# Two engines' score steps moved in the order of the attention stages: ScalarE's exponentials 2.5 steps later, VectorE's maxima 2.5 steps sooner

## The chip, the core and the metric

The kernel is one program on one core of a Trainium2 chip. It is written out by hand: each engine has its own list of instructions, and semaphores alone keep them in step. The metric is the device time in microseconds (us), the median of several runs. In the profile the engines are PE (TensorE matmuls), PEld (TensorE weight loads), DVE (VectorE), ACT (ScalarE), POOL (GpSimd) and SP (SyncE, which issues most DMAs).

## What is computed

Two transformer-like blocks run one after the other on 512 tokens of width 1024, everything in float32 accuracy. The first has sliding-window attention (8 heads), block attention (8 heads; with two key blocks its top-k takes every past block, so it is plain causal attention with a bias), a merge of both, and an MLP. The second has a short convolution, a gated MLP, "forgetting" attention with 16 causal heads, and a second gated MLP. For the change only the two attention stages matter. Their core is, for each head and each tile of 128 queries:

```python
s = einsum(q, k) * scale + bias          # -inf above the diagonal or out of the window
m = max(s, axis=-1)                      # first 8 heads: also max with the head's sink
p = exp(s - m)
p = p / sum(p)                           # first 8 heads: sum(p) + exp(sink - m)
o = einsum(p, v)
```

Stage 1 holds the 8 window heads (kind "swa") and 8 causal heads of the first block, stage 2 the 16 causal heads of the second.

## The kernel before

**Accuracy.** Matmuls run in the type float32r. Each operand is split into a high half (rounded by an ACT copy, `a_hi`) and a low half (the rest, by a DVE subtraction, `d_lo`, `low_half` at L1627), and each product is three matmuls: high by high, high by low, low by high (`mm3`, L598; L599 to L601). So whatever TensorE writes and later reads again passes through ACT first and then DVE.

**One head.** A head has four query tiles. For tile i TensorE writes the scores to one of two PSUM banks (`score` at L724; in stage 2 a fourth matmul at L744 adds the forget gates). DVE adds the bias or mask and takes the row maximum in one instruction (L1663), then makes the negative maximum column (L1668). ACT takes the exponential in place and sums it (L1206). When all four tiles are done, "norm": DVE takes the reciprocal of the sums (L1678) and scales tiles 0 to 2 (L1681), ACT scales tile 3 (L1230). Then come the turnings "t": TensorE transposes 128x128 blocks of probabilities to one of two other banks (L756), ACT makes the high half (L1238), DVE the low half (L1629 through `low_half`). A causal head has four turnings (t.0 of four blocks, t.1 of three, t.2 of two, t.3 of one), a window head two. Then "v": TensorE multiplies them by the values (L772 to L774). Last "out": the head's result is split by ACT (L1244) and DVE (L1629) in the place of its queries. A causal tile i is 128(i+1) keys wide, so its exponential and its maximum go over 128 to 512 columns.

**Banks.** A score bank is free for the score after the next when DVE has taken the maximum (event "top"). A turning bank is free for the turning after the next when DVE has the low half (event "pt"). So t.0 of a head waits for the low half of t.2 of the head before it.

**The order.** `attention_steps` (L209) makes one list of steps for each stage, and TensorE, ACT, DVE and POOL each walk through it and do what in it concerns them: `STEPS1` (L285) and `STEPS2` (L287). Heads overlap: while head n is multiplied, the scores of later heads and the turnings of head n+1 are already made. The order of one head is written out in tables:

```python
SEQ = {"causal": ["v0", "t2", "v1", "t3", "+t0", "v2", "+t1", "v3"],
       "swa": ["v0", "v1", "+t0", "v2", "v3", "+t1"]}
LEAD = {"causal": [8, 8, 8, 9, 10, 11, 12, 12], "swa": [10, 11, 12, 12, 12, 13]}
```

A "+" is a turning of the next head, and LEAD says how many score tiles have been started by then. Between these steps stand units of other work for TensorE (`fill`): projections of the keys, values and gates needed later, each unit one `mm3` of 512 columns or two of 256 (L599 to L601). They end in "evac" steps (ACT's high half, DVE's low half of a whole bank; in between L1185, L1201). "piece" steps convert a quarter of a weight slot, ACT the high part (L1118), POOL the low part (L2042). "start" steps are POOL's (the bias DMA of a head in stage 1, the gate operand at L2100 in stage 2). In stage 2 the work for filling is used up in head 12, so the last heads run without any. A stretch of the list for a causal head with filling reads:

```text
t8.3  score10.0  unit  t9.0  score10.1  unit  v8.2  score10.2  evac  take  unit  piece0
t9.1  score10.3  start12  unit  piece1  v8.3  unit  piece2  v9.0  unit  piece3  norm10  t9.2
```

and of the last ones, without:

```text
norm13  t12.2  out11  v12.1  t12.3  score14.0  t13.0  score14.1  v12.2  score14.2  t13.1
score14.3  v12.3  v13.0  norm14  t13.2  out12  v13.1  t13.3  score15.0  t14.0 ...
```

Units, takes and v are TensorE's alone. Of a "score" step ACT does the exponential, DVE the maximum, TensorE the four matmuls. The engines' loops over the list are the functions `attention` in `program_act` (L1212), `program_dve` (L1684), `program_pe` (L830) and `program_pool` (L2110).

Of the kernel before, what the change touches and what calls it, by code (L numbers as in the profile page):

```python
# [191 lines left out]
def job_units(job):  # L192

    kind, slot = job
    if kind == "o":
        yield ("idle",)
        yield ("take", slot)
        for i in range(2):
            for kt in range(5):
                yield ("unit", job, i, kt)  # L200
        return
    yield ("take", slot)
    for i in range(2):
        for u in range(8):
            yield ("unit", job, i, u)
        yield ("evac", job, i)


def attention_steps(kinds, jobs, quota, first):  # L209


    steps, pieces = [], []
    n_heads = len(kinds)

    def one_unit():
        for job in jobs:
            for step in job_units(job):
                if step[0] == "take":
                    while pieces:
                        steps.append(pieces.pop(0))  # L220
                    steps.append(step)
                    if step[1] + 1 in PIECED and step[1] + 1 >= first:
                        pieces.extend(("piece", step[1] + 1, c) for c in range(4))
                elif step[0] == "evac":
                    steps.append(step)
                else:
                    steps.append(step)
                    yield

    units = one_unit()  # L230

    def fill(n):
        for _ in range(n):
            next(units, None)
            if pieces:
                steps.append(pieces.pop(0))

    started, tiled = [0], [0]

    def start(n):  # L240
        while started[0] < min(n, n_heads):
            steps.append(("start", started[0]))
            started[0] += 1

    def tiles(n):
        while tiled[0] < min(n, 4 * n_heads):
            steps.append(("score", tiled[0] // 4, tiled[0] % 4))
            tiled[0] += 1
            start(tiled[0] // 4 + 2)

    start(2)
    for n in range(8):
        tiles(n + 1)
        fill(1)
    steps.append(("norm", 0))
    fill(1)
    for g in (0, 1):
        steps.append(("t", 0, g))
        fill(1)
    for n, kind in enumerate(kinds):  # L260
        nxt = n + 1 < n_heads
        seq = SEQ[kind]
        extra = max(0, quota[n] - len(seq))
        for at, step in enumerate(seq):
            if at == NORM[kind] and nxt:
                steps.append(("norm", n + 1))
            if at == 2 and n:
                steps.append(("out", n - 1))
            if step[0] != "+":
                steps.append((step[0], n, int(step[1])))  # L270
            elif nxt:
                steps.append((step[1], n + 1, int(step[2])))
            lead = LEAD[kind][at]
            tiles(4 * n + (lead if nxt and kinds[n + 1] == kind else min(lead, 12)))
            fill(2 if at < extra else (1 if at < quota[n] else 0))
    steps.append(("out", n_heads - 1))
    for _ in units:
        pass
    steps.extend(pieces)
    return steps  # L280

# [61 lines left out]
def build(nc, a, out_t, scratch):  # L345
    with ExitStack() as ctx:
# [164 lines left out]
        stage_steps = {1: STEPS1, 2: STEPS2}  # L511
# [564 lines left out]
        def prob(st, h, i):  # L1076
            hd = heads[st][h]
            n, off = score_span(hd, i)[1], OFF[hd["kind"]][i]
            return sp_b[h % 2][:, off:off + n]
# [24 lines left out]
        def program_act(act, on):  # L1104
# [8 lines left out]
            def piece(n, c):  # L1113
                s = slice(512 * c, 512 * c + 512)
                on.wait_ge(raw_in[n % NRAW], "landed", n)
                if n >= NW:
                    on.wait_ge(mm, "slot", n - NW)
                act.activation(WH[:, n % NW, s], raw[:, n % NRAW, s], ACT.Copy).then_inc(w_hi.sem, w_hi.up("slot", n, c))  # L1118
# [68 lines left out]
            def evacuate(name, n, i, bank):  # L1187
                if name[0] == "q":
                    queries(name[:2], 2 * int(name[2]) + i, bank, "job", n, i)
                elif name[0] == "g":  # L1190
                    k = 2 * int(name[1]) + i
                    on.wait_ge(mm, "job", n, i)
                    act.activation(sg_b[k], psum[bank][:, :], ACT.Copy).then_inc(a_evac.sem, a_evac.up("gate", k))
                elif name[-2] == "k":
                    kv_free(on, name)
                    keys(name, bank, n, i)
                else:
                    kv_free(on, name)
                    on.wait_ge(mm, "job", n, i)
                    src, hi, lo = places_of_values(name, bank, i)  # L1200
                    act.activation(hi, src, ACT.Copy).then_inc(a_hi.sem, a_hi.up(name, i))  # L1201
# [9 lines left out]

            def attention(st, tiles_done, turns_done):  # L1212
                tile, turn = tiles_done, turns_done
                for step in stage_steps[st]:
                    what = step[0]
                    if what == "take":
                        slot[0] += 1
                    elif what == "piece":
                        piece(step[1], step[2])
                    elif what == "evac":  # L1220
                        (name, n), i = step[1:]
                        evacuate(name, n, i, 6 + tile % 2)
                        tile += 1
                    elif what == "score":
                        exponentials(st, step[1], step[2])
                    elif what == "norm":
                        h = step[1]
                        on.wait_ge(a_exp, "exp", st, h, 3)
                        on.wait_ge(d_soft, "recip", st, h)
                        act.activation(prob(st, h, 3), prob(st, h, 3), ACT.Copy, scale=stats(h)[4][:, 3:4]).then_inc(  # L1230
                            a_exp.sem, a_exp.up("scaled", st, h, 3))
                    elif what == "t":
                        h, g = step[1:]
                        src, hi, lo = weights_turned(st, h, g, 2 + turn % 2)
                        turn += 1
                        on.wait_ge(mm, "turned", st, h, g)
                        turned_free(on, st, h, g)
                        act.activation(hi, src, ACT.Copy).then_inc(a_hi.sem, a_hi.up("pt", st, h, g))  # L1238
                    elif what == "out":
                        h = step[1]  # L1240
                        hd = heads[st][h]
                        r = slice(hd["r0"], hd["r0"] + 64)
                        on.wait_ge(mm, "sum", st, h, 3)
                        act.activation(hd["q"][0][r, :], psum[4 + h % 2][r, :], ACT.Copy).then_inc(  # L1244
                            a_hi.sem, a_hi.up("out", st, h))
# [243 lines left out]
        def program_dve(dve, on):  # L1489
# [193 lines left out]

            def attention(st, tiles_done, turns_done):  # L1684
                tile, turn, scored = tiles_done, turns_done, 0
                for step in stage_steps[st]:
                    what = step[0]
                    if what == "take":
                        slot[0] += 1
                    elif what == "evac":  # L1690
                        (name, n), i = step[1:]
                        evacuate(name, i, 6 + tile % 2)
                        tile += 1
                    elif what == "score":
                        score(st, step[1], step[2], scored % 2)
                        scored += 1
                    elif what == "norm":
                        normalise(st, step[1])
                    elif what == "t":
                        h, g = step[1:]  # L1700
                        src, hi, lo = weights_turned(st, h, g, 2 + turn % 2)
                        turn += 1
                        low_half(lo, src, hi, "pt", st, h, g)
                    elif what == "out":
                        h = step[1]
                        hd = heads[st][h]
                        r = slice(hd["r0"], hd["r0"] + 64)
                        low_half(hd["q"][1][r, :], psum[4 + h % 2][r, :], hd["q"][0][r, :], "out", st, h)
# [719 lines left out]
```

## Time and profile before

| what | value |
|---|---|
| median of 3 runs | 2031.24 us (2031.15 to 2031.51) |
| the profiled execution | 2031.23 us, of which the span of its instructions 2029.4 us |
| TensorE matmuls busy | 1954.0 us, 96% |
| VectorE, ScalarE, GpSimd busy | 57%, 37%, 16% |
| stage 1 of attention | about 76 to 245 us of the span |
| stage 2 of attention | about 1405 to 1595 us |

The span is the time from the first to the last instruction in the trace; the rest of the execution's time, some 2 us, lies around it. In the rows an engine's idle time stands in front of an instruction together with what ended it: `[1.05 <-ACT t L1238]` means that it stood still 1.05 us until the ACT instruction of L1238 was done.

### The profile page before, as it was taken

The numbers are of one execution on the slowest core, as the hardware profiler recorded it, in microseconds if no ns is written. First come the engines' busy times: TensorE is split into PE (matmuls) and PEld (weight loads), VectorE is DVE, ScalarE is ACT, GpSimd is POOL, SyncE is SP. The second block draws the span as 40 slices with busy tenths as digits, with TensorE's granted clock in tenths as the row PEclk, the third lists the DMA queues.
The fourth block names the chain that finished last, engine by engine and source line by source line (L and its number), as shares of the span: only waits on it lengthen the run. The fifth ranks groups of instructions, "written<-read, shape, count | busy, mean of one in ns | idle before, by whom it ended". The sixth has DMA issues, their size and how long they took to land.

```text
span 2029.4 us, 22573 instructions
## 1 busy us (share of the span) xinstructions
PE 1954.0 (96%) x9134; PEld 1607.5 (79%) x9134; DVE 1163.7 (57%) x1841; ACT 757.0 (37%) x1141; POOL 333.2 (16%) x293
## 2 busy tenths in 40 slices
PE   4999999999999999999999999999999899999997
PEld 3888888778888887887888888868888678888885
DVE  6566565576676745666655654565666554432445
ACT  4556632352223234223422122374565352222223
POOL 4422211021111102003100000147222130000002
PEclk9999999999999999999999999999999999999998
DMA  9422366266565424432654523232111122323321
GB/s 330 138 82 63 114 232 236 83 219 215 210 219 196 166 85 169 161 108 80 237 195 169 187 87 100 86 123 88 43 42 43 64 91 95 104 83 104 98 90 42
DMA packets 126121, 267.57 MB, mean 132 GB/s; under 512 B 4463, under 2 KB 33151, under 8 KB 126016
## 3 DMA queue, kind: packets, MB, share of 16 engines
q1 hardware_dynamic: 121056, 248.59, 35.9%
q0 software_dynamic: 4960, 17.53, 2.4%
q8 instruction: 72, 1.18, 0.2%
q14 instruction: 33, 0.27, 0.0%
HBM read 261.84 MB, written 8.45 MB: 133 GB/s over the span
## 4 chain that ended last, share of the span: by engine, by line
PE 66%; ACT 5%; DVE 4%; POOL 2%; issue 1%; DMA 1%; ACTq 0%; SPq 0%; DVEq 0%; POOLq 0%
PE ps L599 21%; PE ps L601 21%; PE ps L600 21%; DVE t L1629 1%; ACT t L1164 1%; ACT t L1160 1%; ACT t L1206 1%; ACT t L1118 1%; PE ps L756 1%; POOL t L2227 1%; DVE t L1663 1%; DVE t L1601 0%; DVE t L1554 0%; DMA x_keep<-t 0%; POOL t L2042 0%
## 5 line engine op out<-in xcount | busy, mean ns | idle before, releaser
L599 PE MATMUL ps<-t 128*128 128x512 f32 (+1 forms) x2504 | 969.5, 387 | 17.5 <-DVE t L1629 4.3
L601 PE MATMUL ps<-t 128*128 128x512 f32 (+1 forms) x2504 | 962.8, 385 | 0.0
L600 PE MATMUL ps<-t 128*128 128x512 f32 (+1 forms) x2504 | 962.0, 384 | 0.0
L599 PEld LDWEIGHTS ps<-t 128*128 128x128 f32 x2504 | 471.4, 188 | 119.0 <-DVE t L1494 6.5
L1494 DVE TENSOR_TENSOR t<-t 128x2048 fp32r<-128x2048 f32 x133 | 305.0, 2294 | 441.9 <-ACT t L1111 441.9
L601 PEld LDWEIGHTS ps<-t 128*128 128x128 f32 x2504 | 470.9, 188 | 98.9
L600 PEld LDWEIGHTS ps<-t 128*128 128x128 f32 x2504 | 471.2, 188 | 94.2 <-issue 1.0
L1111 ACT ACTIVATE t<-t 128x2048 fp32r<-128x2048 f32 x133 | 254.3, 1912 | 618.6 <-PE ps L601 611.1
L1554 DVE SCALAR_TENSOR_TENSOR t<-ps,t 128x512 f32<-128x512 f32 x184 | 132.6, 748 | 91.5 <-PE ps L601 82.7
L1506 DVE CUSTOM_DVE_ANT_0 t<-t 128x1024 f32<-128x1024 f32 x144 | 175.5, 1260 | 10.3 <-DMA t<-in_ada_t 3.6
L1629 DVE TENSOR_TENSOR t<-ps,t 64x512 fp32r<-64x512 f32 (+4 forms) x183 | 103.8, 577 | 103.4 <-ACT t L1238 48.7
L2042 POOL TENSOR_TENSOR t<-t 128x512 fp32r<-128x512 f32 x88 | 117.1, 1346 | 221.9 <-ACT t L1118 221.9
L2071 POOL COPY t<-t 128x512 f32<-128x512 f32 x4 | 2.8, 710 | 849.1 <-DVE t L1554 801.6
L1206 ACT ACTIVATE t<-t 128x256 f32<-128x256 f32 (+3 forms) x128 | 69.4, 542 | 118.2 <-DVE t L1668 117.1
L1629 DVE TENSOR_TENSOR t<-t 128x512 fp32r<-128x512 f32 (+1 forms) x93 | 71.1, 767 | 73.1 <-ACT t L1392 30.7
L2178 POOL TENSOR_TENSOR t<-t 128x512 f32<-128x512 f32 x32 | 46.3, 1446 | 282.2 <-ACT t L1331 282.2
L1134 ACT ACTIVATE t<-t 128x512 f32<-128x512 f32 x56 | 35.0, 631 | 89.9 <-DVE t L1554 88.2
L756 PE MATMUL ps<-t 128*128 128x128 f32 x296 | 53.2, 279 | 12.9 <-DVE t L1629 11.4
L1392 ACT ACTIVATE t<-t 128x512 fp32r<-128x512 f32 x44 | 27.8, 632 | 99.9 <-DVE t L1907 99.9
L1663 DVE CUSTOM_DVE_ANT_0 t<-ps,t 128x256 f32<-128x256 f32 (+3 forms) x128 | 58.4, 456 | 8.8 <-PE ps L744 6.1
L756 PEld LDWEIGHTS ps<-t 128*128 128x128 f32 x296 | 37.0, 141 | 25.4 <-DVE t L1629 15.1
L1160 ACT ACTIVATE t<-t 128x512 fp32r<-128x512 f32 x56 | 45.2, 807 | 27.7 <-DVE t L1618 14.1
(170 smaller groups left out, 1561.8 us busy)
## 6 DMA issues: line engine op xcount, KB each, us to landing
t<-in_ada SPq DMA_DIRECT2D x48, 1024.0 KB, 6.0
t<-in_gate SPq DMA_DIRECT2D x22, 1024.0 KB, 5.0
t<-in_up SPq DMA_DIRECT2D x22, 1024.0 KB, 5.1
t<-in_down SPq DMA_DIRECT2D x22, 1024.0 KB, 5.1
t<-in_w_in SPq DMA_DIRECT2D x17, 1024.0 KB, 5.7
t<-in_w_mlp_in SPq DMA_DIRECT2D x16, 1024.0 KB, 5.4
t<-in_w_mlp_out SPq DMA_DIRECT2D x16, 1024.0 KB, 5.1
t<-in_ada_t POOLq DMA_DIRECT2D x13, 1024.0 KB, 6.0
```

The source lines that it names most:

```text
L599: pe.matmul(o, wh, xh, start=first, stop=False)
L600: pe.matmul(o, wh, xl, start=False, stop=False)
L601: return pe.matmul(o, wl, xh, start=False, stop=last)
L756: ins = pe.transpose(psum[bank][:, blocks[n]], sp_b[h % 2][:, col:col + P], ident)
L1111: act.activation(WH[:, n % NW, :], raw[:, n % NRAW, :], ACT.Copy).then_inc(w_hi.sem, w_hi.up("slot", n))
L1206: act.activation(prob(st, h, i), prob(st, h, i), ACT.Exp, bias=neg[:, i:i + 1], accum_out=sm[:, i:i + 1]).then_inc(a_exp.sem, a_exp.up("ex ...
L1494: dve.tensor_tensor(WL[:, n % NW, :], raw[:, n % NRAW, :], WH[:, n % NW, :].bitcast(F), ALU.subtract).then_inc(w_lo_d.sem, w_lo_d.up("slot ...
L1506: ins = dve.tensor_tensor_reduce(out=v, in0=v, in1=cs, scale=1.0, scalar=0.0, op0=ALU.mult, op1=ALU.add, accum_out=mods[:, col + i:col + i ...
L1554: return dve.scalar_tensor_tensor(out=X[k], in0=psum[bank][:, :], scalar=gate, in1=X[k], op0=ALU.mult, op1=ALU.add)
L1629: dve.tensor_tensor(lo, src, hi.bitcast(F), ALU.subtract).then_inc(d_lo.sem, d_lo.up(*event))
L1663: dve.tensor_tensor_reduce(out=prob(st, h, i), in0=psum[bank][:, 0:n], in1=bias_of(st, h, i), scale=1.0, scalar=LOW, op0=ALU.add, op1=ALU. ...
L2042: pool.tensor_tensor(WL[:, n % NW, s], raw[:, n % NRAW, s], WH[:, n % NW, s].bitcast(F), ALU.subtract).then_inc(w_lo_p.sem, w_lo_p.up("slo ...
```

## The change

Both engines' loops walk through a sorted copy of the list. A score step counts 2.5 places later for ScalarE and 2.5 sooner for VectorE; every other step keeps its number, and TensorE and GpSimd keep the old list.

```diff
+def moved(steps, by):
+
+    return [step for _, step in sorted(enumerate(steps), key=lambda e: e[0] + by.get(e[1][0], 0))]
...
             def attention(st, tiles_done, turns_done):
                 tile, turn = tiles_done, turns_done
-                for step in stage_steps[st]:
+                for step in moved(stage_steps[st], {"score": 2.5}):
                     what = step[0]
...
             def attention(st, tiles_done, turns_done):
                 tile, turn, scored = tiles_done, turns_done, 0
-                for step in stage_steps[st]:
+                for step in moved(stage_steps[st], {"score": -2.5}):
                     what = step[0]
```

The first of the two is in `program_act`, the second in `program_dve`. The same instructions with the same operands are issued.

## Rows read from the trace of the kernel before

**Rows 1.** The page, busy time of each engine over the span

```profile
PE 1954.0 (96%) x9134; PEld 1607.5 (79%) x9134; DVE 1163.7 (57%) x1841; ACT 757.0 (37%) x1141; POOL 333.2 (16%) x293
```

**Rows 2.** Waits of PE, 76 to 245 us: us in total, times, longest

```profile
PE ps L756 <- DVE t L1629: 1.9, 3, 1.0
PE ps L756 <- DVE t L1681: 1.4, 3, 0.6
PE ps L738 <- DVE t L1663: 1.1, 2, 0.6
PE ps L772 <- DVE t L1629: 1.0, 2, 0.7
```

**Rows 3.** Waits of PE, 1405 to 1595 us

```profile
PE ps L756 <- DVE t L1629: 9.5, 8, 2.5
PE ps L738 <- DVE t L1663: 1.8, 2, 1.0
PE ps L599 <- DVE t L1629: 1.6, 1, 1.6
PE ps L772 <- DVE t L1629: 1.2, 3, 0.6
```

**Rows 4.** Waits of PE, 1562 to 1592 us, the last heads

```profile
PE ps L756 <- DVE t L1629: 5.5, 3, 2.5
```

**Rows 5.** Waits of ACT and of DVE, 1405 to 1595 us

```profile
ACT t L1206 <- DVE t L1668: 62.8, 53, 2.3
...
DVE t L1629 <- ACT t L1238: 27.9, 41, 1.5
```

**Rows 6.** Timeline of the last heads: start us, us, instruction, [idle before <-releaser]

```profile
1565.64 0.66 PE L756 MATMUL ps<-t 128*128 128x128 f32 x4 [1.00 <-DVE t L1629]
1569.32 0.50 PE L738 MATMUL ps<-t 128*128 128x512 f32 x1 [0.95 <-DVE t L1663]
1575.27 0.66 PE L756 MATMUL ps<-t 128*128 128x128 f32 x4 [2.02 <-DVE t L1629]
1584.63 0.99 PE L756 MATMUL ps<-t 128*128 128x128 f32 x4 [2.49 <-DVE t L1629]
...
1565.77 1.02 DVE L1629 TENSOR_TENSOR t<-ps,t 64x512 fp32r<-64x512 f32 x2 [0.19 <-ACT t L1244]
1568.23 0.69 DVE L1629 TENSOR_TENSOR t<-ps,t 128x512 fp32r<-128x512 f32 x1 [1.05 <-ACT t L1238]
1571.26 0.56 DVE L1629 TENSOR_TENSOR t<-ps,t 128x384 fp32r<-128x384 f32 x1 [1.15 <-ACT t L1238]
1571.73 0.68 DVE L1663 CUSTOM_DVE_ANT_0 t<-ps,t 128x512 f32<-128x512 f32 x1
1573.71 0.88 DVE L1681 TENSOR_SCALAR t<-t 128x128 f32<-128x128 f32 x3
```

**Rows 7.** Timeline of PE, two stalls in heads with filling

```profile
1486.78 0.44 PE L756 MATMUL ps<-t 128*128 128x128 f32 x2 [1.20 <-DVE t L1629]
...
1521.10 0.66 PE L756 MATMUL ps<-t 128*128 128x128 f32 x4 [0.58 <-DVE t L1629]
```

**Rows 8.** Timeline of DVE, 1479 to 1485 us, ahead of the first of them

```profile
1479.83 1.41 DVE L1629 TENSOR_TENSOR t<-ps,t 64x512 fp32r<-64x512 f32 x2 [1.26 <-ACT t L1185]
...
1482.10 0.68 DVE L1663 CUSTOM_DVE_ANT_0 t<-ps,t 128x512 f32<-128x512 f32 x1
...
1484.07 1.92 DVE L1681 TENSOR_SCALAR t<-t 128x128 f32<-128x128 f32 x3
```

**Rows 9.** Timeline of DVE in a window head of stage 1, low half of out

```profile
123.74 0.68 DVE L1629 TENSOR_TENSOR t<-ps,t 64x512 fp32r<-64x512 f32 x1 [1.58 <-ACT t L1244]
```

**Rows 10.** A stretch: us, busy (x count) of five engines, PEclk, DMA, GB/s

```profile
1586.00:1588.00 2.00, 2.00 (x10) 1.90 (x9) 1.23 (x2) 0.74 (x2) 0.00 (x0) 0.50 0.00 0
```

**Rows 11.** Line 1681 (ns min/median/max), and timeline of POOL beside that scaling

```profile
L1681 DVE TENSOR_SCALAR t<-t x96: 285/348/1468, 85.0 to 1583.5; 128x256 f32<-128x256 f32 x40, 128x128 f32<-128x128 f32 x32, 128x384 f32<-128x384 f32 x24
...
1484.43 3.94 POOL L2042 TENSOR_TENSOR t<-t 128x512 fp32r<-128x512 f32 x3 [1.31 <-ACT t L1118]
```

## The prediction

> **What bounds the kernel now.** I read the page's busy times first, then who TensorE waits for in the two attention stages, then the timeline of each engine around those waits. TensorE matmuls cover 1954.0 of 2029.4 us [rows 1], so only 75 us in the whole kernel are open, and the change touches the stretches 76 to 245 us (stage 1) and 1405 to 1595 us (stage 2). There TensorE waits for VectorE and next to nothing else: 5.4 us in stage 1 [rows 2] and 14.1 us in stage 2 [rows 3], of which 5.5 us are one kind of stall in the last three heads, where no projection work is left to fill in [rows 4]. That is 19.5 us at most for any reordering. VectorE and ScalarE are not full in these stages, they wait for each other: in stage 2 ScalarE stands 62.8 us before exponentials (L1206) until VectorE has the negative maximum (L1668), and VectorE 27.9 us before low halves (L1629) until ScalarE has the high half (L1238) [rows 5]. Both queues are in order, so a step that waits holds all that stands behind it.
>
> **The ping-pong, in the last heads.** [rows 6] shows one cycle of a head without filling, from one "t.0" turning on TensorE to the next: 1565.64, then 1575.27, 9.63 us. On VectorE the low half of t.0 (1568.23) waits 1.05 us for a high half that ScalarE does only behind the exponential of tile 0, and the maxima of tiles 1 and 2 stand behind it. The same again at tile 3: the low half of t.1 (1571.26) waited 1.15 us, maximum 3 follows at 1571.73, then exponential, reciprocal and scaling (1573.71, 0.88 us), the low half of t.2, and the next turning. TensorE stalls 0.95 us for a score bank (1569.32) and 2.02 us for that last step.
>
> **What the change moves.** Nothing is added or removed; no DMA moves (SP's loads, POOL's loads and its order are untouched). Steps are sorted by place, a score step counted 2.5 later for ScalarE and 2.5 sooner for VectorE, while TensorE and POOL keep their order. Most of what is passed is TensorE's alone, so the order of an engine changes only where a step of its own is passed. Written out from the plan: on ScalarE 26 of 64 exponentials in stage 1 (passing 11 weight pieces, 6 t, 6 evac, 3 norm) and 30 of 64 in stage 2 (17 t, 11 evac, 2 pieces); on VectorE 41 maxima in stage 1 (33 t, 8 norm, 7 out) and 42 in stage 2 (42 t). A causal head's VectorE order goes from t.3, s.0, t.0, s.1, s.2, t.1, s.3 to s.0, t.3, s.1, t.0, s.2, s.3, t.1; ScalarE's becomes t.3, t.0, s.0, s.1, t.1, s.2, s.3 in the last heads. Each engine then has work that is ready while the other does the half it needs.
>
> **Last heads, step by step** (differences of starts in [rows 6]). Take the same turning at 1565.64. VectorE's low half of "out" starts at 1565.77 and maximum 3 at 1571.73, 5.96 us later. In between lie the two waits (1.05 and 1.15) and the low half of t.1 (0.48 to the next start), and all three now come off the path to maximum 3, as the high halves are done while VectorE takes maxima: 5.96 - 2.68 = 3.28, so VectorE could take it at 1569.05. Score 3 has to be there: its bank is now freed before TensorE asks, the 0.95 us go, it starts at 1568.4, and four 512-column matmuls take it to about 1569.5 (0.50 for the first, 0.23 between starts: an estimate). Maximum 3 at 1569.5 for 1571.73 is 2.2 us sooner. What follows it, 3.5 us to the turning, stays as it is. The cycle becomes 7.4 us for 9.63, with 0.8 us of stall left for 2.02. Two such cycles (the second ends at 1584.63 behind 2.49 us of stall) give 4.4 us. The 1.00 us in front of them loses about 0.5, as in the filled heads below. Term: -4.9.
>
> **Filled causal heads.** The stalls are at the same step, t.0 behind the low half of t.2: 1.20 us at 1486.78 and 0.58 at 1521.10 [rows 7], five stalls and 4.0 us before the last heads (9.5 less 5.5 us, 8 less 3) [rows 3, 4]. In [rows 8] maximum 3 starts at 1482.10 behind the low half of t.1. Put first, it starts when the two low halves of the evacuation are through (1479.83 + 1.41), 0.86 us sooner, and its exponential, the scaling and t.2 move along. So 1.20 becomes 0.34, another long one alike, and the shorter ones nearly vanish. Term for stage 2: -3.1. In stage 1's causal heads the three stalls of this kind sum to 1.9 us, the longest 1.0 [rows 2]; by the same 0.86 they come to 0.2: -1.7.
>
> **Window heads of stage 1.** Two stalls of a score bank, 1.1 us [rows 2], arise as maximum 0 stands behind the low half of t.1; passing it is worth the 0.48 of [rows 6] to each: -1.0. Three stalls for the scaling, 1.4 us: maximum 1 now goes ahead of norm and costs it some 0.6, but maximum 3 goes ahead of out and t.0. The low half of out waited 1.58 us, until 123.74, for ScalarE [rows 9], and out and t.0 take about 1.2 on VectorE before maximum 3: that much sooner is all that comes after. I take half of the 1.4: -0.7.
>
> **What it costs.** 75 low halves of turned weights come later by a maximum and its column (0.68 us for the widest alone [rows 6], less than half for the narrowest), and may wait for a score first. The weighted products need them; the stalls of that kind are 1.0 and 1.2 us now [rows 2, 3]. The cover is TensorE's own projection work (a unit of three 512-column matmuls) between t and v. In the last heads, where it is missing, the low half of t.1 lands at about 1570.8, just as TensorE reaches the product that needs it. I put +0.4, bounds 0 and +3. Weight pieces go ahead of exponentials in 13 places: they only come sooner. Work behind attention (output projection, the reload of x, the next weight slot) starts from its end and shifts with it: 0.
>
> **The clock.** The granted clock is 0.50 in 1586 to 1588 [rows 10], the lower of its two levels (1.2 of 2.4 GHz), right behind the longest stall, 2.49 us [rows 6]; behind the one of 2.02 us four transposes take 0.66 us, so it was still high. With that stall near 0.8 the fall may not come. The four transposes take 0.99 us there for 0.66, half as much again; over 3.8 us of work at that pace it is at most 1.3 us. Bounds 0 and -1.3; as no row decides, half: -0.6.
>
> **Sum.** -4.9 - 3.1 - 1.7 - 1.0 - 0.7 + 0.4 - 0.6 = -11.6. The profiled execution took 2031.23 us (span 2029.4), the median is 2031.24, so no correction: **2019.6 us**.
>
> **A rule that speaks against it.** VectorE's scaling (L1681, three tiles) takes 1.92 us at 1484.07, where POOL's pieces run (3.94 us from 1484.43), and 0.88 us at 1573.71 without them [rows 6, 8, 11]. The Trainium skill, "SBUF — State Buffer", section "Who interferes with whom", has VectorE and GpSimd contending for a shared port pair as an exclusive lock in such cases. Hanging on that, the trace agrees in kind: the op lengthens only beside POOL.
>
> **The rivals.**
> (a) *The stalls re-form, 14%.* TensorE arrives sooner, and the same chain (exponential 3, reciprocal, scaling, t.2) ends last again with less gained. For: the scaling chain is untouched, 3 us of it. Against: it starts from maximum 3, which the order does bring forward. Only half the last-head term would stay: 2031.2 - 2.5 = 2028.7.
> (b) *Scalings fall beside POOL, 5%.* The 96 instructions go from 285 to 1468 ns [rows 11], and by the timeline 13 of the 32 scalings are long now. If the 12 short ones outside the first and last heads became long, 12 x 1.04 (1.92 less 0.88) = 12.5 on the chain: 2019.6 + 12.5 = 2032. Against: pieces and scaling hang on the same exponential and move together. It is the skill's lock rule that would drive it.
> (c) *Slower, 7%.* VectorE stands before a maximum whose score TensorE has not written (its queue is in order), with a low half behind it that v or a turning needs. Price: maximum and column, about 0.6, plus a score of four matmuls, about 0.7: 1.3 us. It decides where the cover between t and v is under 1.3 us, less than two units. If half of the 32 heads lost 1 us against now, +16 less the last heads' gain: 2031.2 + 16 - 4.9 = about 2042; with a quarter of them 2034, which I take.
> (d) *Forecast, 74%.* The step orders follow from the sort, so the change does what it says; that case gets no chance of its own.
>
> **Numbers.** A difference of about 0.2% (4 us) is what can be told from none. Below 2027.2: forecast and a fifth of (a), 0.77; within: the rest of (a) and (b), 0.16; above: 0.07. Floor: all 19.5 us and 1.3 of clock would be 2010; with half of the forecast's leftover stalls gone too, 2014. Upwards the range goes into (a): 2028.5.
>
> **What would show it.** Right: ScalarE's wait at L1206 for L1668 in stage 2 well under 62.8 us and VectorE's at L1629 for L1238 under 27.9, VectorE's waits at L1663 for scores up; the last heads' cycle near 7.4 us; L738 stalls gone; stalls at L756 for L1629 of stage 2 under 4. Wrong: new stalls at L772 for L1629, waits of TensorE equal to now, or L1681 longer in the mean.

## The result, and the profile after

The changed kernel takes **2011.57 us** in the median (2010.2 to 2012.88, 4 runs) against 2031.2: a ratio of 0.9902, 95% interval 0.9888 to 0.9916, so 19.6 us or 1% faster. The forecast was 2019.6, and 2014.0 to 2028.5 does not hold it. The direction and the mechanism of the moves were right; the gain was two thirds larger than forecast, as each stall was priced too low.

First where it lies. The span fell from 2029.4 to 2010.3 us. Taking each stage from its first score matmul to its last product by values, stage 1 went from 167.1 us (75.8 to 242.9) to 159.6, stage 2 from 185.0 (1406.0 to 1591.0) to 173.7; all the rest of the kernel together lost 0.4. The rows are those of the two lines for each stage, with the first and the last start; only the matmul rows stand here. The kernel before, lines 738 and 774:

```profile
L738 PE MATMUL ps<-t x64: 277/364/496, 75.8 to 230.7; 128*128 128x256 f32 x48, 128*128 128x384 f32 x8, 128*128 128x512 f32 x8
L774 PE MATMUL ps<-t x64: 273/281/397, 88.0 to 242.9; 128*128 128x256 f32 x32, 128*128 128x128 f32 x16, 128*128 128x512 f32 x8, 128*128 128x384 f32 x8
...
L738 PE MATMUL ps<-t x64: 277/364/504, 1406.0 to 1578.7; 128*128 128x256 f32 x32, 128*128 128x384 f32 x16, 128*128 128x512 f32 x16
L774 PE MATMUL ps<-t x64: 273/336/419, 1423.6 to 1591.0; 128*128 128x512 f32 x16, 128*128 128x384 f32 x16, 128*128 128x256 f32 x16, 128*128 128x128 f32 x16
```

The changed kernel, lines 743 (first matmul of a score) and 779 (last of a product), in stage 1 and in stage 2:

```profile
L743 PE MATMUL ps<-t x64: 277/362/487, 74.6 to 222.0; 128*128 128x256 f32 x48, 128*128 128x384 f32 x8, 128*128 128x512 f32 x8
L779 PE MATMUL ps<-t x64: 273/281/397, 86.8 to 234.2; 128*128 128x256 f32 x32, 128*128 128x128 f32 x16, 128*128 128x512 f32 x8, 128*128 128x384 f32 x8
...
L743 PE MATMUL ps<-t x64: 277/364/482, 1398.6 to 1562.2; 128*128 128x256 f32 x32, 128*128 128x384 f32 x16, 128*128 128x512 f32 x16
L779 PE MATMUL ps<-t x64: 273/308/397, 1416.3 to 1572.3; 128*128 128x512 f32 x16, 128*128 128x384 f32 x16, 128*128 128x256 f32 x16, 128*128 128x128 f32 x16
```

(Lines of the changed kernel stand five further down than those of the kernel before.) TensorE's waits in stage 1 (74 to 236 us), where [rows 2] had 5.4 us. The first is of the projections ahead of it:

```profile
PE ps L889 <- ACT t L1287: 0.8, 1, 0.8
PE ps L777 <- DVE t L1634: 0.3, 1, 0.3
PE ps L761 <- DVE t L1686: 0.2, 1, 0.2
```

and in stage 2 (1398 to 1575 us), where [rows 3] had 14.1:

```profile
PE ps L777 <- DVE t L1634: 2.5, 7, 0.6
PE ps L761 <- DVE t L1634: 2.2, 3, 1.2
PE ps L604 <- DVE t L1634: 1.6, 1, 1.6
```

The stalls before turnings (9.5 us) are down to 2.2, those for a score bank are gone, and those before products have doubled from 1.2 to 2.5: the price of low halves that come later. ScalarE's and VectorE's own waits in the same stretch, against [rows 5]:

```profile
ACT t L1243 <- PE ps L761: 29.5, 32, 1.6
ACT t L1211 <- DVE t L1673: 22.3, 44, 2.3
...
DVE t L1668 <- PE ps L749: 31.2, 45, 1.8
DVE t L1634 <- ACT t L1243: 7.9, 18, 0.9
```

ScalarE waited 62.8 us for negative maxima and now 22.3; VectorE waited 27.9 for high halves and now 7.9. In their place both wait for TensorE, ScalarE 29.5 us for turnings and VectorE 31.2 for scores. TensorE's own waits for VectorE are down from 14.1 to 6.3 us in the same stretch.

Last, one cycle of the last heads, to be read beside [rows 6]:

```profile
1559.93 0.66 PE L761 MATMUL ps<-t 128*128 128x128 f32 x4 [0.77 <-DVE t L1634]
...
1566.96 0.66 PE L761 MATMUL ps<-t 128*128 128x128 f32 x4 [1.23 <-DVE t L1634]
...
1560.53 0.27 DVE L1668 CUSTOM_DVE_ANT_0 t<-ps,t 128x128 f32<-128x128 f32 x1
1560.92 0.28 DVE L1634 TENSOR_TENSOR t<-ps,t 128x128 fp32r<-128x128 f32 x1
1561.12 0.41 DVE L1668 CUSTOM_DVE_ANT_0 t<-ps,t 128x256 f32<-128x256 f32 x1
1561.64 0.68 DVE L1634 TENSOR_TENSOR t<-ps,t 128x512 fp32r<-128x512 f32 x1
1562.24 0.55 DVE L1668 CUSTOM_DVE_ANT_0 t<-ps,t 128x384 f32<-128x384 f32 x1
1563.41 0.69 DVE L1668 CUSTOM_DVE_ANT_0 t<-ps,t 128x512 f32<-128x512 f32 x1 [0.43 <-PE ps L749]
1564.22 0.55 DVE L1634 TENSOR_TENSOR t<-ps,t 128x384 fp32r<-128x384 f32 x1
1565.40 0.88 DVE L1686 TENSOR_SCALAR t<-t 128x128 f32<-128x128 f32 x3
```

(VectorE's read-outs and negative maxima between these rows, and the reciprocal, are left out.) Maxima and the low halves of t.0 and t.1 alternate without a wait for ScalarE, maximum 3 waits only for its score, and the cycle is 7.03 us for 9.63.

### The profile page after: what moved, and what is told of

Its sections match the earlier page's. It is cut to its first block, busy times and chain, and to the rows that moved or that the text cites. A ratio compares the mean times of both kernels' runs of the same rounds, so it can differ in the third digit from the quotient of the medians.

```text
span 2010.3 us, 22573 instructions
## 1 busy us (share of the span) xinstructions
PE 1947.9 (97%) x9134; PEld 1605.5 (80%) x9134; DVE 1166.7 (58%) x1841; ACT 758.5 (38%) x1141; POOL 333.2 (17%) x293
## 3 DMA queue, kind: packets, MB, share of 16 engines
HBM read 261.84 MB, written 8.45 MB: 134 GB/s over the span
## 4 chain that ended last, share of the span: by engine, by line
PE 69%; ACT 4%; DVE 3%; POOL 2%; issue 1%; DMA 1%; ACTq 0%; SPq 0%; DVEq 0%; POOLq 0%
PE ps L604 21%; PE ps L606 21%; PE ps L605 21%; ACT t L1165 1%; ACT t L1169 1%; PE ps L761 1%; POOL t L2232 1%; DVE t L1634 1%; PE ps L743 1%; PE ps L744 1%; PE ps L749 1%; PE ps L745 1%; PE ps L777 0%; DVE t L1606 0%; DVE t L1559 0%
## 5 line engine op out<-in xcount | busy, mean ns | idle before, releaser
L604 PEld LDWEIGHTS ps<-t 128*128 128x128 f32 x2504 | 470.8, 188 | 117.8 <-DVE t L1499 6.5
L606 PEld LDWEIGHTS ps<-t 128*128 128x128 f32 x2504 | 470.9, 188 | 98.9
L605 PEld LDWEIGHTS ps<-t 128*128 128x128 f32 x2504 | 471.0, 188 | 94.4 <-issue 1.0
L2047 POOL TENSOR_TENSOR t<-t 128x512 fp32r<-128x512 f32 x88 | 116.9, 1346 | 203.1 <-ACT t L1123 203.1
L1634 DVE TENSOR_TENSOR t<-ps,t 64x512 fp32r<-64x512 f32 (+4 forms) x183 | 104.3, 574 | 39.2 <-ACT t L1243 14.8
L1243 ACT ACTIVATE t<-ps 128x512 fp32r<-128x512 f32 (+1 forms) x112 | 50.0, 448 | 50.0 <-PE ps L761 49.2
```

What stands on the lines that cost most here:

```text
L604: pe.matmul(o, wh, xh, start=first, stop=False)
L605: pe.matmul(o, wh, xl, start=False, stop=False)
L606: return pe.matmul(o, wl, xh, start=False, stop=last)
L1634: dve.tensor_tensor(lo, src, hi.bitcast(F), ALU.subtract).then_inc(d_lo.sem, d_lo.up(*event))
L2047: pool.tensor_tensor(WL[:, n % NW, s], raw[:, n % NRAW, s], WH[:, n % NW, s].bitcast(F), ALU.subtract).then_inc(w_lo_p.sem, w_lo_p.up("slo ...
```

## The experiments

Two questions were open: which of the two moves does it, and why the gain is so much larger than TensorE's idle time allowed. For each run the two stages are measured as above, from the trace, together with TensorE's idle time in them (the gaps between the end of one matmul and the start of the next, summed). The stages came out very steadily: the changed kernel ran again later with 159.6 and 173.7. The last column has the times from one t.0 turning to the next, for the last two heads.

| kernel | median us | ratio (95% interval) | stage 1, idle | stage 2, idle | last two cycles |
|---|---|---|---|---|---|
| before | 2031.2 | | 167.1, 5.4 | 185.0, 14.5 | 9.63, 9.36 |
| changed | 2011.6 | 0.9902 (0.9888 to 0.9916) | 159.6, 0.7 | 173.7, 6.5 | 7.03, 7.03 |
| changed, again | 2012.0 | 0.9908 (0.9895 to 0.9922) | 159.6, 0.7 | 173.7, 6.4 | 7.03, 7.05 |
| ScalarE's move alone | 2023.0 | 0.9963 (0.9951 to 0.9976) | 167.6, 5.6 | 177.6, 8.3 | 7.74, 7.59 |
| VectorE's move alone | 2012.3 | 0.9906 (0.9891 to 0.9921) | 159.4, 0.6 | 174.1, 6.9 | 7.38, 7.11 |
| both, stage 1 alone | 2023.5 | 0.9964 (0.9952 to 0.9977) | 159.7, 0.7 | 184.1, 14.8 | 9.64, 9.36 |
| both, stage 2 alone | 2017.4 | 0.9935 (0.9923 to 0.9948) | 167.1, 5.5 | 173.7, 6.4 | 7.03, 7.03 |
| VectorE, 1.5 sooner | 2012.0 | 0.9902 (0.9887 to 0.9917) | 160.2, 0.7 | 174.2, 6.8 | 7.38, 7.11 |
| VectorE, 1.5, tile 3 only | 2014.6 | 0.9921 (0.9907 to 0.9935) | 160.4, 1.0 | 176.8, 8.3 | 8.45, 8.18 |
| VectorE, 1.5, tiles 0 and 1 | 2024.7 | 0.9973 (0.9964 to 0.9982) | 165.9, 4.1 | 181.6, 10.9 | 8.90, 9.85 |
| changed, VectorE 3.5 | 2010.2 | 0.9895 (0.9881 to 0.9908) | 159.6, 0.7 | 173.5, 5.9 | 7.49, 7.10 |
| the same, again | 2011.6 | 0.9905 (0.9892 to 0.9919) | 159.7, 0.7 | 173.5, 5.9 | 7.48, 7.11 |
| changed, norm 1.5 later | 2020.5 | 0.9948 (0.9935 to 0.9961) | 162.3, 2.7 | 180.9, 9.6 | 7.36, 7.08 |
| changed, one turning bank | 2036.1 (one run) | | 165.5, 4.6 | 192.7, 16.5 | 9.20, 9.71 |

The kernel before took 2030.4 to 2031.4 us in the median beside these. In stage 1 the granted clock is 1.00 in every one of these traces. Stage 2 holds a fall to 0.50 in five: before and with ScalarE's move alone behind the last long stall (0.73 and 0.74 in the mean from there to the end), with tiles 0 and 1 for some 7 us, most of them in the cycle of 9.85, with norm later for some 3.5 us near its start, and with one turning bank in three places. Their times for stage 2 hold what that cost, 0.9 us in the kernel before (worked out below).

### Each engine's move alone

```diff
 # act_only: in program_dve
-                for step in moved(stage_steps[st], {"score": -2.5}):
+                for step in stage_steps[st]:
 # dve_only: in program_act
-                for step in moved(stage_steps[st], {"score": 2.5}):
+                for step in stage_steps[st]:
```

> Only ScalarE's exponentials move (2.5 later); VectorE keeps the old order. Theory D (VectorE's move carries the gain: maxima no longer stand behind low halves that wait for ScalarE): the last heads gain about 1.7 us per cycle, as the high half of t.0 no longer waits for the exponential of tile 0, the filled heads nothing, the window heads about 1.5 us; in all about -6 us (2025). Theory S (the two moves only work together, each engine needs ready work): under a third each, -3 to -6 us for this one and the same for the other. Theory A (ScalarE's move carries it): -15 us or more.

> Only VectorE's maxima move (2.5 sooner); ScalarE keeps the old order. Theory D: nearly all of the gain, -15 to -18 us (2013 to 2016), last-head cycle near 7.2 us. Theory S: -3 to -6 us. Theory A: about -5 us, and TensorE's waits for a low half (L1634) as long as before.

VectorE's move alone has the whole gain within the runs' spread (0.9906 for 0.9902) and ScalarE's alone 7.9 us, all of it in stage 2. Theory D held, theories S and A fell; its number for ScalarE alone was off in parts. In stage 1 nothing came of the 1.5 us named for the window heads: TensorE's waits for the scaling rose there from 1.4 to 3.2 us. In stage 2 the last three cycles gave the 5.1 us named, but the filled heads gave 2.5 us where nothing was expected. TensorE's waits in stage 2 with ScalarE's move alone (1395 to 1590 us):

```profile
PE ps L761 <- DVE t L1634: 5.2, 5, 2.1
PE ps L604 <- DVE t L1634: 1.6, 1, 1.6
PE ps L777 <- DVE t L1634: 1.1, 3, 0.6
```

and with VectorE's alone (1398 to 1580 us):

```profile
PE ps L777 <- DVE t L1634: 3.5, 7, 0.8
PE ps L761 <- DVE t L1634: 1.6, 3, 1.0
PE ps L604 <- DVE t L1634: 1.5, 1, 1.5
```

The two moves break the same chain (7.4 and 10.9 us in stage 2 alone, 11.3 together), so they don't add up. With VectorE moved, what ScalarE's adds in the stages is 0.4 us in stage 2 and -0.2 in stage 1, too little for the whole-kernel times to tell.

### Each stage alone

```diff
 # stage1_only; stage2_only has st == 2. ScalarE's line alike, with 2.5
-                for step in moved(stage_steps[st], {"score": -2.5}):
+                for step in moved(stage_steps[st], {"score": -2.5 if st == 1 else 0}):
```

> Both moves, in stage 1 alone. Theory P (a stall of TensorE costs its idle time in the trace plus about 0.25 us that the modelled matmul ends hide, so the stalls undercount the loss): -7.5 us, although TensorE's stalls there sum to 5.4 us before and 0.7 after. Theory V (the idle time is the loss, and what is beyond it came from the clock or from other parts of the program): -4.7 us.

> Both moves, in stage 2 alone. Theory P: -11 to -12 us, of which about 1 is the fall of the clock behind the last stall. Theory V: -8 us. If the stages are independent, this and the run with stage 1 alone add up to the whole change, -19.6 us.

Stage 1 alone shortens its stage by 7.4 us where the idle time fell by 4.7; stage 2 alone by 11.3 where it fell by 8.1. The other stage stays as it was (167.1; 184.1 for 185.0, of which more below). Theory V, that idle time is the loss, falls. The medians, 7.3 and 13.5 us under the kernel before, sum to 20.8 against 19.6 of the whole: independent within the spread. (The 13.5 hold 2.2 us more than the stage shows, which lie outside it.)

### Which maxima

```diff
 # dve_narrow: VectorE alone
-                for step in moved(stage_steps[st], {"score": -2.5}):
+                for step in moved(stage_steps[st], {"score": -1.5}):
 # dve_tile3 and dve_tiles01: the same, with tiles (3,) or (0, 1)
-def moved(steps, by):
+def moved(steps, by, tiles):
...
-key=lambda e: e[0] + by.get(e[1][0], 0))]
+key=lambda e: e[0] + (by.get(e[1][0], 0) if e[1][0] != "score" or e[1][1] > 1 and e[1][2] in tiles else 0))]
```

> VectorE's maxima 1.5 steps sooner instead of 2.5, ScalarE as before: 33 and 42 maxima still pass a turning's low half, but none passes norm or out. Theory D1 (passing the turnings is what counts): as the run with VectorE alone, 2012 +- 2. Theory D2 (in the window heads the gain comes from maximum 3 ahead of out and maximum 1 ahead of norm): stage 1 gives back 3 us or more, 2015 to 2016, stage 2 unchanged.

> VectorE alone, 1.5 steps sooner, and only the maxima of tile 3 (from head 2 on): 14 pass the low half of t.1 in stage 1 and 14 in stage 2. The prediction's steps: in the filled causal heads this one order carries the gain, so stage 2 loses its long stalls (about 1.2 us, twice) and the last heads' cycle comes from 9.6 to about 8.4, as the wait for the high half of t.0 stays; stage 2 from 185.0 to about 178, stage 1 from 167.1 to about 163; kernel about 2020. If tiles 0 and 1 carry it, under 3 us of gain.

> The complement: only the maxima of tiles 0 and 1 (19 in stage 1, 28 in stage 2 pass a low half). By the prediction's steps nothing in the filled causal heads, 1 us a cycle in the last heads and the score-bank stalls of the window heads: stage 2 to about 182, stage 1 to about 165.5, kernel about 2026. If tiles 0 and 1 carry the gain, 2015 or less. If the two sets do not add up to the 19 us of both, the order works as a whole.

With 1.5 the maxima pass only turnings' low halves, and all of the gain is there but 0.8 us of stage 1. So passing norm and out, to which the prediction gave the window heads' scaling stalls, is worth under 1 us. In the two other runs the maxima move from head 2 on, 28 of tile 3 in the one and 47 of tiles 0 and 1 in the other; those of tile 2 pass no turning. Tile 3's have the most: 6.7 us in stage 1 and 8.2 in stage 2. Their waits in stage 2 (1390 to 1600 us) against the complement's:

```profile
PE ps L777 <- DVE t L1634: 2.5, 7, 0.6
PE ps L761 <- DVE t L1634: 2.2, 3, 1.2
PE ps L743 <- DVE t L1668: 1.9, 2, 1.0
PE ps L604 <- DVE t L1634: 1.5, 1, 1.5
```

```profile
PE ps L761 <- DVE t L1634: 7.1, 9, 2.0
PE ps L777 <- DVE t L1634: 2.0, 4, 0.8
PE ps L604 <- DVE t L1634: 1.5, 1, 1.5
```

Tile 3 alone leaves the two stalls for a score bank (L743, 1.9 us) and shortens those before turnings, 9.5 us in the kernel before, to 2.2 (the complement leaves 7.1). Tiles 0 and 1 remove the two for a score bank and leave long ones before turnings, but not in the filled heads: there the two stalls of 1.2 us came down to 0.5, where the prediction's steps said nothing would change. The last heads' cycle of 8.45 is the 8.4 that was expected; the complement's is 8.90 for the 8.6 expected, and its last one, 9.85 with the clock at 0.50 in much of it, is no shorter than before. The two sets sum to 7.9 us in stage 1 and 11.6 in stage 2, for 6.9 and 10.8 of both together: nearly additive, as far as the clock lets it be told. Wrong besides is stage 1 for tile 3: 160.4 for the 163 expected.

### Further the same way, and the chain behind it

```diff
 # dve_35, dve_35_again
-                for step in moved(stage_steps[st], {"score": -2.5}):
+                for step in moved(stage_steps[st], {"score": -3.5}):
 # norm_later, on both engines (ScalarE's line with 2.5)
-                for step in moved(stage_steps[st], {"score": -2.5}):
+                for step in moved(stage_steps[st], {"score": -2.5, "norm": 1.5}):
```

> ScalarE as in the change, VectorE's maxima 3.5 steps sooner: 9 of them also pass an evacuation and 4 more a turning. If passing more is better, 1 us less; if a maximum in front of an evacuation holds a projection bank, TensorE's new stalls are at the projections and the kernel is 1 to 3 us slower than the changed one.

> ScalarE 2.5 later, VectorE 3.5 sooner, beside the changed kernel. If it is better it has a lower median by 1 us or more (2010.5 against 2011.6 in the runs so far) with stage 2 at 173.5; if that was the clock's place, the two agree within 1 us.

> The changed kernel once more, beside the next one on the same chip: 2011 to 2013. Its attention stages within 0.2 us of 159.6 and 173.7; what differs from the first time lies in where the clock falls outside them, 1 to 3 us.

> On top of the change norm moves 1.5 steps later on ScalarE and VectorE, behind t.2 of the head before (causal heads only): high and low half of t.2 are made while the exponential of tile 3 runs. If the chain exponential 3, reciprocal, scaling, low half of t.2 sets the last heads' cycle, it falls from 7.03 to about 6.5 us, two or three times, and the kernel gains 1 to 1.5 us (2010.3). If scaling alone is what the next turning waits for, it stays at 7.03, or grows by the 0.36 us that t.2 now takes ahead of it.

Farther than 2.5 is a plateau: 0.2 us in stage 2, and beside each other 2011.6 and 2012.0. No version tried is better than the changed one by more than the spread. Moving norm behind t.2 missed what was expected of it: it is 8.9 us slower than the change. TensorE's waits in stage 2 (1385 to 1590 us) and VectorE's longest there:

```profile
PE ps L761 <- DVE t L1686: 5.1, 5, 2.9
...
DVE t L1634 <- ACT t L1243: 31.7, 19, 3.0
```

About half of the loss is a side effect that the expectation did not name. In both stages the sort also puts norm of head 0 behind an evacuation, on both engines, so the first turning of the stage waits for a scaling (L1686) that comes after the evacuation's low half:

```profile
1415.93 1.03 PE L761 MATMUL ps<-t 128*128 128x128 f32 x4 [2.91 <-DVE t L1686]
```

Behind this one the granted clock was 0.50 for some 3.5 us, and stage 1 begins with one of 2.0 us. The first heads of stage 2 take 3.2 us more than in the changed kernel, of 7.2 for the whole stage, and most of stage 1's 2.7 us lies at its own first turning. What is left for norm behind t.2 is 4 us of stage 2: 1.2 in the heads with filling, 2.1 in the last three cycles and 0.6 behind them. There the low half of t.2, now ahead of the scaling, waits for a high half (31.7 us in all for 7.9), and turnings wait for the scaling. That would be the same fault as the one that the change removes, ready work queued behind work that is not; no run shows it without the move of norm 0.

### The price of a stall

```diff
 # one_turn_bank: the same in program_act and program_dve
-                        transposes(st, step[1], step[2], 2 + turn[0] % 2)
+                        transposes(st, step[1], step[2], 2)
```

> The changed kernel with one PSUM bank for turnings instead of two, so that nearly every turning waits for the low half of the one before: many stalls of TensorE of a known kind. Theory P (a stall costs its idle time plus about 0.35 us): with n added stalls the two attention stages grow by the added idle time plus 0.35 n; for 80 added stalls 28 us more than the idle time shows. Theory V: they grow by the idle time alone, within 2 us.

Only 25 stalls were added, 11 and 14, not 80. Stage 1 grew by 5.9 us where the idle time grew by 3.8 over 11 stalls, 0.19 us a stall more than the trace shows. In stage 2 (19.0 us for 10.0) the clock also fell, in three places, so that figure is no clean one. Theory P has the right sign and half its size here; over all kernels in the table, stage 1 against the changed kernel reads: before 7.5 us for 4.7 of idle time, ScalarE alone 8.0 for 4.9, tiles 0 and 1 6.3 for 3.4, one bank 5.9 for 3.8, norm later 2.7 for 2.0. Each us of shown idle time stands for 1.4 to 1.9 us.

Why can be read from the kernels' own rows. The kernel before, the last matmul ahead of the stall that [rows 6] has at 1575.27:

```profile
1572.97 0.28 PE L744 MATMUL ps<-t 128*128 128x256 f32 x1
```

and the changed kernel, two score matmuls and what follows them without a stall:

```profile
1560.66 0.28 PE L745 MATMUL ps<-t 128*128 128x256 f32 x1
1560.78 0.28 PE L749 MATMUL ps<-t 128*128 128x256 f32 x1
1560.90 0.28 PE L777 MATMUL ps<-t 128*128 128x256 f32 x1
```

Matmuls in a row start 0.12 us apart but each is shown for 0.28 (the profile models the ends of matmuls): they overlap. So TensorE could have started the turning at 1573.09 and did at 1575.27, 2.18 us lost, where the idle time, counted from the end at 1573.25, says 2.02. Every stall is short by this overlap of 0.16 us, the same within 0.01 for matmuls of 128, 384 and 512 columns, and one that is shorter shows no idle time at all.

Counted that way for every matmul of the two stages (start to next start, less 0.23, 0.18, 0.12 or 0.11 us for 512, 384, 256 or 128 columns, the spacing in a row, where that is positive), the lost time fell from 14.7 to 7.6 us in stage 1 and from 24.6 to 14.6 in stage 2 up to the last t.0 turning: 17.1 us. The idle time of the same stretches fell by 13.0 (5.4 to 0.7, 13.9 to 5.6). Of the 4.1 us between, 1.5 lie at matmuls that show no gap, and 2.6 in the overlap of those that do. The stretches themselves became 17.8 us shorter; the 0.7 that is left this count does not place.

## Why the prediction was wrong

- **"That is 19.5 us at most for any reordering"**: this is the step that failed, and with it the price of every term, for each stall was put at the idle time that the trace shows before it. The stages lost 18.7 us, with 7.2 us of idle time still there. The sum of idle times is a lower bound of what stalls cost, not an upper one. Up to the last t.0 turning the idle time fell by 2.2 us in the window heads, 2.5 in the causal heads of stage 1, 3.1 in the filled heads and 5.2 in the last ones, 13.0 for 11.4 forecast (1.7, 1.7, 3.1, 4.9). So 1.6 us are stalls that went further than forecast, 4.1 are the overlap that this unit leaves out, 0.7 stay without a place, and the clock gave 0.9 for 0.6: together the 6.7 us between the 12.0 forecast and 18.7.
- **Last heads, -4.9**: right mechanism. The cycles that were to become 7.4 are 7.03; measured from turning to turning the three went from 9.89, 9.63 and 9.36 to 8.35, 7.03 and 7.03, 6.5 us. The two later ones lost 2.1 us of idle time each, near the 2.2 forecast, but 2.6 and 2.3 us of time. The stall of 1.00 in front of them, put at half, went whole, and its cycle lost 1.5 us for 0.5. Maximum 3 waits for nothing but its score, as said.
- **Filled causal heads of stage 2, -3.1**: measured 3.9. The two heads with long stalls (1.20 and 1.19) went from 12.68 to 11.24 us each, 1.44 for a forecast of 0.86. The two stalls of 0.58, said nearly to vanish, are gone by name and not in time: their heads took 11.89 and 11.88 and take 11.87 and 11.88, as a product now waits instead:

```profile
1463.49 0.44 PE L777 MATMUL ps<-t 128*128 128x384 f32 x1 [0.47 <-DVE t L1634]
```

- **Causal heads of stage 1, -1.7**: measured 3.6. The term left out the stalls before products (1.0 us), of which one of 0.66 went too.
- **Window heads, -1.0 and -0.7**: measured 3.7 over four heads that took 41.0 us and take 37.3. Halving the second term was wrong: the scaling stalls went, and, by the run with 1.5 steps, not because of norm and out but because of maxima ahead of turnings. The trace had this order to show (maxima 1 to 3 behind a low half that waits), and I weighed it for the causal heads alone.
- **Cost, +0.4**: right in kind. Stalls before products in stage 2 rose from 1.2 to 2.5 us.
- **The clock, -0.6**: the stage with the old order took 185.0 us with the fall of the clock behind its last stall, and 184.1 without one in the run with stage 1 alone, so it cost 0.9. A stretch of 6 us about the same turning (1577.21 there, 1584.63 in the kernel before), in that run:

```profile
1577.00:1583.00 6.00, 4.95 (x30) 3.88 (x31) 3.69 (x8) 2.78 (x8) 0.00 (x0) 1.00 0.00 0
```

and in the kernel before:

```profile
1584.00:1590.00 6.00, 5.07 (x24) 4.48 (x25) 3.33 (x7) 3.09 (x8) 0.00 (x0) 0.72 0.00 0
```

(The stretch and its us, then busy us and count of PE, PEld, DVE, ACT and POOL, the granted clock, the DMA share and GB/s.) The same order and the same last stall of 2.49 us, once with the clock at 1.00 throughout and once at 0.72 in the mean. Counted from the turning itself 6 us hold 30 matmuls and 25, and up to the last product it is 5.4 us for 6.3. So the bounds of 0 to 1.3 held, 0.6 was fair, and a stall of that length does not by itself decide whether the clock falls. How much of the 0.9 the change earned, and how much it would have had by chance, is therefore open.

- **The sum.** Window heads 3.8 (with 0.1 of the first heads), causal heads of stage 1 3.6, filled heads of stage 2 3.9, last heads 6.5, clock 0.9: 18.7 us, for 12.0 forecast before the cost of 0.4. Outside the stages 0.4 us more went (stage 1 starts 1.2 us sooner, the stretch between the stages is 1.3 longer, the end 0.5 shorter), 19.1 us of span in all.
- **Rival (a)**, stalls that re-form, came only in its small form, the two of 0.58 us above. **Rival (b)**, scalings beside POOL, did not come:

```profile
L1686 DVE TENSOR_SCALAR t<-t x96: 285/348/1459, 83.8 to 1565.9; 128x256 f32<-128x256 f32 x40, 128x128 f32<-128x128 f32 x32, 128x384 f32<-128x384 f32 x24
```

The mean is 485 ns for 480, and 11 of the 32 scalings are long (over 1.3 us for three tiles) for 13. But pieces and scaling did not just move together, as was said there. In stage 1 two scalings that took 1.87 us or more came clear of POOL, one that took 1.84 takes 2.62, and one of 1.92 takes 3.56:

```profile
214.62 3.56 DVE L1686 TENSOR_SCALAR t<-t 128x128 f32<-128x128 f32 x3
```

TensorE waited 0.09 us behind the first and not at all behind the second. So the lock rule of the Trainium skill ("SBUF — State Buffer", "Who interferes with whom") had something to act on, in few places and with TensorE covered; the trace agrees with it in that all 11 long ones lie beside a POOL instruction of L2047 and none of the short ones does. **Rival (c)**, VectorE before a score that is not written, is there in full as a wait (31.2 us in stage 2, for 6.1 before) and cost next to nothing: 1.3 us more before products. The low halves behind those maxima had their cover.
- **The signs.** Those named for right all came: ScalarE's wait 22.3 for 62.8, VectorE's 7.9 for 27.9, its waits for scores up from 6.1 to 31.2, no stall for a score bank, the last cycle 7.03, stalls before turnings 2.2 (under 4). Of those named for wrong one came in part, the products' stalls, worth 1.3 us in stage 2 (in stage 1 they fell from 1.0 to 0.3); L1686's mean rose by 5 ns, 0.5 us in all.

## What to carry to other kernels

Where matmuls overlap in the profile, as here (0.12 us apart, 0.28 shown), TensorE's summed idle time is a floor and no ceiling for what a reordering can win: measure from start to start, or one whole cycle of the loop from turning to turning, before and after. Where two in-order engines wait for each other in turn, put ahead those steps that need only the third engine, where that one is mostly done by then; moving VectorE's maxima alone broke the chain as well as moving both. Then look at what the steps that now come late hold up, and at every step that a sort moves, the first head's too, as the run with norm moved shows.

## What the runs showed of the hardware

- The attention stages repeat far better than the whole kernel: 159.62 and 159.63 us, 173.73 and 173.71, in two profiled executions of the same kernel on different occasions, while their spans are 2010.3 and 2006.4 us. The difference lies outside, much of it behind attention, where the end took 438.0 us in the one and 435.6 in the other. One place is behind a wait of TensorE of 2.91 us, right after attention, which both have. In the changed kernel, and run again:

```profile
1603.28 0.50 PE L604 MATMUL ps<-t 128*128 128x512 f32 x1 [2.91 <-DVE t L1499]
```

```profile
1601.76 0.50 PE L604 MATMUL ps<-t 128*128 128x512 f32 x1 [2.91 <-DVE t L1499]
```

Behind it the granted clock fell in the one and not in the other, at the same work (columns as above). The changed kernel:

```profile
1604.00:1608.00 4.00, 4.00 (x13) 3.09 (x12) 2.18 (x3) 3.97 (x5) 3.18 (x2) 0.57 0.82 266
```

and the same, run again:

```profile
1602.00:1606.00 4.00, 4.00 (x18) 3.22 (x18) 2.67 (x4) 3.57 (x5) 3.25 (x2) 1.00 0.77 246
```

TensorE was busy throughout in both stretches; 13 matmuls in 4 us at a clock of 0.57, 18 at 1.00. With the stall of 2.49 us above this is the second place where the clock fell behind a stall in one trace and not behind the same stall in another. So a difference of 1 or 2 us between versions is told by the stages and not by the whole.
- What a stall of TensorE costs, as worked out above: its shown idle time and 0.16 us of overlap, and up to the overlap where no idle time shows.
